# Computing the adaLN modulation of a two-layer hybrid backbone with the weight blocks stationary

## The reference, cut to what matters

```python
mod = jax.nn.silu(cond) @ ada_w + ada_b          # ada_w: (1024, 3072) per layer, float32
shift, scale, gate = jnp.split(mod, 3, axis=-1)
h = rms_norm(x, norm_g) * (1.0 + scale[:, None, :]) + shift[:, None, :]
# ... h @ w_in feeds a gated recurrence, a differential attention and a Fourier mixer ...
x_new = x + gate[:, None, :] * (merged @ w_out)
```

## Time and profile before

| what | value |
|---|---|
| median of 3 runs | 3388.12 us (3386.97 to 3388.16) |
| the profiled execution's own time | 3383.91 us |
| its span, first to last instruction | 3381.9 us |
| mean granted clock of TensorE | 0.979 |
| PE busy | 3139.2 us, 93% |
| PEld busy | 2976.2 us, 88% |
| DVE, ACT, POOL busy | 1296.2, 1073.8, 690.0 us |

### The profile page before, as it was taken

One profiled execution on the slowest core, in us unless ns is written; L12 is line 12 of the kernel. 1 busy time (PEld: TensorE's weight loads), 2 busy tenths in 40 slices (PEclk: granted clock), 3 DMA queues, 4 the chain that ended last, 5 costly groups with the idle time before them and its releaser, 6 DMA issues.

```text
span 3381.9 us, 43875 instructions
## 1 busy us (share of the span) xinstructions
PE 3139.2 (93%) x18496; PEld 2976.2 (88%) x18496; DVE 1296.2 (38%) x1769; ACT 1073.8 (32%) x2022; POOL 690.0 (20%) x404
## 2 busy tenths in 40 slices
PE   5798889899999999999988988989999999999999
PEld 1388888898898999999988888979889899999999
DVE  1253455356564211121335445435656431022121
ACT  1332333356654311010123333345656432011010
POOL 0021112111111123333331111111111112233332
PEclk9899999999999999999999999999999999999999
DMA  8301000100101111211330100110000020121131
GB/s 321 126 26 42 30 30 27 50 21 28 36 22 48 55 32 47 66 46 40 131 122 27 36 30 27 34 50 21 29 30 22 26 76 29 47 67 46 41 110 68
DMA packets 52115, 182.58 MB, mean 54 GB/s; under 512 B 5584, under 2 KB 12752, under 8 KB 49232
## 3 DMA queue, kind: packets, MB, share of 16 engines
q1 hardware_dynamic: 28800, 92.29, 8.9%
q10 hardware_dynamic: 23120, 87.49, 6.8%
HBM read 149.35 MB, written 30.41 MB: 53 GB/s over the span
## 4 chain that ended last, share of the span: by engine, by line
PE 80%; DVE 9%; ACT 5%; DVEq 3%; issue 2%; ACTq 1%; DMA 1%
PE ps L319 59%; PE ps L530 3%; PE ps L373 3%; PE ps L504 2%; PE ps L505 2%; PE ps L517 2%; DVE a_at L1291 1%; PE ps L421 1%; DVE stat L1407 1%; DVEq L1283 1%; PE ps L586 1%; PE ps L468 1%; DVE a_q L1280 1%; ACT a_at L808 1%; DVE b_qs L1387 1%
## 5 line engine op out<-in xcount | busy, mean ns | idle before, releaser
L319 PE MATMUL ps<-h_hi,w_hi 128*128 128x384 f32 x3648 | 1240.2, 340 | 50.3 <-DVE h_lo L1237 25.7
L319 PE MATMUL ps<-h_hi,w_lo 128*128 128x384 f32 x3648 | 1225.6, 336 | 0.0
L319 PE MATMUL ps<-h_lo,w_hi 128*128 128x384 f32 x3648 | 1225.2, 336 | 0.0
L319 PEld LDWEIGHTS ps<-h_hi,w_hi 128*128 128x128 f32 x3648 | 690.0, 189 | 59.6 <-issue 58.0
L679 POOL CAST w_hi<-w_raw 128x1024 fp32r<-128x1024 f32 x200 | 197.2, 986 | 2650.4 <-PE ps L319 2645.4
L319 PEld LDWEIGHTS ps<-h_hi,w_lo 128*128 128x128 f32 x3648 | 690.0, 189 | 2.0 <-issue 1.0
L319 PEld LDWEIGHTS ps<-h_lo,w_hi 128*128 128x128 f32 x3648 | 689.7, 189 | 0.0
L681 POOL TENSOR_TENSOR w_lo<-w_raw,w_hi 128x1024 fp32r<-128x1024 f32 x200 | 492.6, 2463 | 16.0
L1074 ACT ACTIVATE m_g<-ps 128x384 f32<-128x384 f32 x144 | 70.7, 492 | 763.7 <-PE ps L319 753.7
L1407 DVE TENSOR_REDUCE stat<-ps 128x1 f32<-128x1152 f32 (+1 forms) x144 | 177.8, 1235 | 227.9 <-PE ps L505 227.9
L1489 DVE TENSOR_TENSOR m_p<-ps,m_g 128x384 f32<-128x384 f32 x96 | 53.5, 558 | 476.3 <-PE ps L319 476.3
(11 more groups left out here) (218 smaller groups left out, 3567.5 us busy)
## 6 DMA issues: line engine op xcount, KB each, us to landing
w_raw<-in_w_full SPq DMA_DIRECT2D x152, 512.0 KB, 3.5
ada_slabs<-in_ada_w ACTq DMA_DIRECT2D x16, 1536.0 KB, 8.8
w_raw<-in_w_half SPq DMA_DIRECT2D x48, 256.0 KB, 2.6
x_res<-x_keep ACTq DMA_DIRECT2D x16, 576.0 KB, 8.1
out_x_new<-X ACTq DMA_DIRECT2D x16, 576.0 KB, 2.8
X<-in_x_t ACTq DMA_DIRECT2D x1, 4608.0 KB, 18.0
x_keep<-X ACTq DMA_DIRECT2D x1, 4608.0 KB, 13.3
y_keep<-X ACTq DMA_DIRECT2D x8, 576.0 KB, 3.0
```

The costliest lines, as they stand in the source:

```text
L319: mm = pe.matmul(ps[:, bank, 0:TILE], w[:, slot, k, :], r[:, k, cols_of(t)], start=(k == 0 and i == 0), stop=(k == kt - 1 and i == 2))
```

## The change

The operands of the modulation's matmuls are exchanged. A 128x128 block of the slab is stationary, and the two columns of `cond` move. Output block j of layer l lands at once with its channels on the partitions, in columns 2j and 2j + 1 of bank 6 + l, where the 24 blocks of the layer accumulate over its eight slabs. For each slab there are 24 matmuls in place of six. The copies to `mod_row`, the transposes, the buffer, and the semaphores `ada_row`, `ada_t` and `setup_done` go, and with them PE's wait between the layers. DVE waits for `ada_mm` at 8 and 16.

```diff
-    mod_row = at("mod_row", [2, 3 * D_MODEL], F32, off_s + 1024)
...
             for l in range(DEPTH):
-                if l:
-                    pe.wait_ge(ada_row, l)
                 for k in range(KD):
                     s = l * KD + k
                     pe.wait_ge(slab_in[s % 6], 16 * (s // 6 + 1))
-                    for n in range(6):
-                        mm = pe.matmul(ps[0:2, n, :], cond[:, k, :], slabs[:, s % 6, n * 512:(n + 1) * 512],
-                                       start=(k == 0), stop=(k == KD - 1))
+                    for j in range(3 * KD):
+                        mm = pe.matmul(ps[:, 6 + l, 2 * j:2 * j + 2], slabs[:, s % 6, j * P:(j + 1) * P],
+                                       cond[:, k, :], start=(k == 0 and j == 0), stop=(k == KD - 1 and j == 3 * KD - 1))
                     mm.then_inc(ada_mm, 1)
-                pe.wait_ge(ada_row, l + 1)
-                if l:
-                    pe.wait_ge(setup_done, l)
-                for j in range(3 * KD):
-                    mm = pe.transpose(ps[:, 6, 2 * j:2 * j + 2], mod_row[0:2, j * P:(j + 1) * P],
-                                      sq_c[0:2, IDENT, 0:2])
-                mm.then_inc(ada_t, 1)
...
                 if s >= 6:
                     act.wait_ge(ada_mm, s - 5)
-                if s == KD + 5:
-
-                    act.activation(mod_row[:, :].rearrange("p (a b) -> p a b", a=6), ps[0:2, 0:6, :],
-                                   ACT.Copy).then_inc(ada_row, 1)
                 act.dma_start(slabs[:, s % 6, :], ada_w[s // KD, (s % KD) * P:(s % KD + 1) * P, :]).then_inc(slab_in[s % 6], 16)
-            act.wait_ge(ada_mm, DEPTH * KD)
-            act.wait_ge(ada_t, 1)
-            act.activation(mod_row[:, :].rearrange("p (a b) -> p a b", a=6), ps[0:2, 0:6, :],
-                           ACT.Copy).then_inc(ada_row, 1)
             act.wait_ge(lb_sub, 1)
...
-                dve.wait_ge(ada_t, l + 1)
+                dve.wait_ge(ada_mm, KD * (l + 1))
                 ab = par[:, PC_AB + l * 24:PC_AB + (l + 1) * 24].unsqueeze(2).broadcast_to((P, 24, 2))
-                dve.tensor_tensor(mod[:, l, :, :], ps[:, 6, 0:48].rearrange("p (j c) -> p j c", c=2), ab,
-                                  ALU.add).then_inc(setup_done, 1)
+                dve.tensor_tensor(mod[:, l, :, :], ps[:, 6 + l, 0:48].rearrange("p (j c) -> p j c", c=2), ab,
+                                  ALU.add)
```

More of the change, by code:

```diff
@@ L229, in mixer_kernel @@
         tile_free = [sem(f"tile_free{t}") for t in range(NT)]
-        cond_ready, ada_mm, ada_row, ada_t, setup_done, eps_set = (
-            sem(n) for n in ("cond_ready", "ada_mm", "ada_row", "ada_t", "setup_done", "eps_set"))
+        cond_ready, ada_mm, eps_set = (sem(n) for n in ("cond_ready", "ada_mm", "eps_set"))
         lam_dot, lam_exp, lb_sub, lb_exp = (sem(n) for n in ("lam_dot", "lam_exp", "lb_sub", "lb_exp"))
```

## The result

The changed kernel took 3448.33 us (median of 4 runs, 3448.22 to 3448.86) against 3387.57 us before (4 runs, 3386.97 to 3388.16). The ratio is 1.0182, with a 95% interval of 1.0170 to 1.0194: 60.8 us slower, where 64.0 us were forecast.

What follows compares the result with a forecast made beforehand. PE, busy 93% of the span, was taken as the bound. At half clock 163.8 + 0.3 + 0.8 = 164.9 us replace 100.9 us, +64.0 us: 3388.1 us becomes 3452.1 us, range 3438 to 3470 us.

Steps and rivals of the forecast that it cites:

- The price of a pair: Modulation stream on PE: each of 768 load-and-matmul pairs takes 0.2133 us at half clock, 163.8 us in all.
- The nearest rows: Trace streams of ordinary 128x128 blocks, 128 columns moving, taken as pace: 0.1115 us at full, 0.213 us at half clock.
- The reading of the loads' durations: PE loads: above a fixed part, an ordinary float32 block takes 106 ns, a transposing one 53 ns.
- The 337 ns of the upper bound: Modulation stream: if no load hid behind a matmul, each pair takes the load's 337 ns at half clock, 259 us.
- the rival built on it: Modulation stream: float32 loads cost no more than transposing ones; skill's 107 ns gives 82 us; 13.0 us less, chance 0.04.
- The clock: PE's granted clock: begins the modulation stream at 0.50 and stays there until the first projection.
- the likeness to the two-column transposes: Modulation stream looks like the transposes, at 0.50 throughout 142 to 144 us, so its clock would not rise.
- What was removed: Between layers and in the tail: copies, transposes, exponentials leave the path, up to 14.0 us; 0.8 us stay.
- their cover at about 5 us: Tail: lbt to lam_n and layer 0's mod hide under the last slabs' matmuls; uncovered they would cost 5 us.
- What moved: DMA: x_keep, 13.3 us, is issued earlier beside the last slabs; costed at nothing, with 32 us of cover.
- the carry-over to the median: Whole kernel: the profiled execution's 4.2 us under the median is carried over, so 3388.1 + 64.0 = 3452.1 us.
- the uncertainty that the prediction named: Later in the kernel: stretches at 0.50 may fall elsewhere against the work, some us either way.

Runs made afterwards that it cites:

- half_load: The changed kernel loading only 64 columns of each 128x128 block, the other 64 channels' modulation left at the bias; 3370.57 us, ratio 0.9948 to the kernel before.
- wide64: The changed kernel with 64 columns moving in each modulation matmul, 62 of them zeros; 3453.34 us, ratio 1.0191 to the kernel before.
- old_exp_early: The kernel before with ACT's two exponentials moved ahead of its wait for the last slab; 3381.52 us, ratio 0.9983 to the kernel before.
- warm_start: The changed kernel with eight unread float32 matmuls of 384 columns on PE ahead of the stream; 3444.14 us.
- exp_late: The changed kernel with ACT's exponentials put back behind the last slab; 3450.78 us in one execution.
- wide64_warm: wide64_filled with eight matmuls of 384 columns put ahead of the stream; 3371.20 us in one execution.
- wide128: The changed kernel with 128 filled columns moving, six banks a layer, layer 1 waiting for DVE's read, exponentials earlier; 3373.93 us, ratio 0.9959 to the kernel before.
- wide16: The changed kernel with 16 columns moving in each modulation matmul; 3452.15 us in one execution.
- packed: Against the changed kernel: condition stationary again, each slab's six matmuls spread over three column groups, one copy and eight transposes a layer, exponentials early; 3339.02 us.
- packed_early: packed with three slabs' modulation ahead of the norm's sums, SiLU ahead of the squares, slabs 6 to 8 issued earlier; 3331.76 us, ratio 0.9834 to the kernel before.
- wide64_filled: wide64 with the two condition columns repeated 32 times in place of zeros; 3452.34 us in one execution.

## Why the prediction was right, point by point

*The price of a pair* was the whole question, and it was 0.2135 us for 0.2133 forecast; the stream 163.98 us for 163.8. The nearest rows, streams of ordinary blocks with 128 columns moving at half clock, were the right ones. `half_load` and `wide64` show why they carry over: the load's columns set the pace, and 2 or 64 columns moving behind it do not. The arithmetic was looser than it reads, though. The two starts in the earlier trace rows give (262.91 - 262.48) / 2 = 0.215 us and not 0.213; the 0.2133 that was multiplied is 256 cycles at 1.2 GHz and stands in no row. With 0.215 the stream would have been forecast at 165.1 us, 1.1 us too long.

*The reading of the loads' durations* held for the float32 blocks: 64 columns at 0.50 are 0.107 us, which is 128 cycles at 1.2 GHz, two for each column. That a transposing block takes half of that was read from its rows alone; no run tested it. The 337 ns of the upper bound was taken for a load at half clock, which the earlier trace rows do not say; the changed kernel's loads last 333 ns at 0.50. The Trainium skill's figure (TensorE: Matmul & The Clock Gate, section "LDWEIGHTS (loading the stationary operand)") gives, as an estimate, 53 ns for these 64 columns and 107 ns for 128; for float32 blocks the trace shows twice that at 0.50 and about that at 1.00, so the rival built on it fell.

*The clock* stayed at 0.50 from the start of the stream to the projection, as forecast. That it began there was read from the kernel before, with the same idle time ahead. That it would not rise was argued from the likeness to the two-column transposes, and the row that this rested on does not carry it: by the window of 142 to 144 us the clock had long fallen, while PE sat idle, and in `old_exp_early` the same 24 transposes ran at 1.00. The fall at 91 us, with idle time and transposes ahead of it, left both causes open. The first two lines are of the kernel before, the last two of `old_exp_early`:

```profile
139.00:140.00 1.00, 0.00 (x0) 0.00 (x0) 0.70 (x7) 0.00 (x0) 0.00 (x0) 0.71 1.03 419
140.00:141.00 1.00, 0.00 (x0) 0.00 (x0) 0.81 (x7) 0.00 (x0) 0.00 (x0) 0.50 0.99 401
...
136.00:137.00 1.00, 0.66 (x11) 0.67 (x11) 0.00 (x0) 0.28 (x1) 0.00 (x0) 1.00 1.01 401
137.00:138.00 1.00, 0.97 (x16) 0.89 (x15) 0.00 (x0) 0.00 (x0) 0.00 (x0) 1.00 1.03 419
```

So here the forecast was right with some luck. What it claimed was shown only afterwards, by `warm_start`: with two columns moving the level falls without any idle time. The advice of the same page of the Trainium skill (section "Why this matters for your kernels") that continuous work gives TensorE its full clock is not borne out by this stream, which ran at 0.50 for 164 us without a gap.

*What was removed* came out as forecast: 0.82 us between the last matmul and `n_t` for 0.8. That `lbt` to `lam_n` and the `mod` of layer 0 hide is in the trace (they end by 151 us). I priced their cover at about 5 us, which was too much: `exp_late` gives 3.0 us in this kernel, and `old_exp_early` 4.0 us in the kernel before, without the transposes' clock.

*What moved* cost nothing that the trace shows; `x_keep` took 18.1 us to land in place of 13.3, with nobody waiting.

*The term that was off most* is the carry-over to the median. The profiled execution before lay 4.2 us under its median, and I added that to the forecast; that of the changed kernel, 3448.22 us, lies with the rest of its runs. Against the trace the forecast was 3447.9 us for 3448.2, against the median 3452.1 for 3448.33. The +64.3 us between the profiled executions is +60.8 us between the medians, and the 64.0 us lie so near to the first of them because the two profiled executions have nearly the same part behind `n_t` (3237.3 and 3238.0 us).

Where such differences come from can be read in part. Behind `n_t` the clock stood at 0.50 for 123 to 126 us of the traces of the kernel before, `old_exp_early`, `wide64_warm` and `wide128`, whose rest lasts 3236.8 to 3238.7 us, and for 143 to 148 us of `wide64`, `wide16`, `packed` and `packed_early`, whose rest lasts 3241.0 to 3243.9 us. Likewise the executions of the kernel before that took under 3386 us have a mean clock of 0.979 or 0.980, and those above 3389 us one of 0.975 to 0.977. That is the uncertainty that the prediction named (stretches at 0.50 that fall elsewhere). What decides it is not shown.

What stays open is why the streams differ. Of those that started at 0.50, the ones with 2, 16 and 64 columns moving stayed there and the one with 128 rose, as did the stream of the kernel before with 512 (0.69 in its window of 46 to 48 us); of those that started at 1.00, the one with 2 fell and the one with 64 stayed. `warm_start` and `wide64_warm` are one execution each. No rule follows from them.

## What to carry to other kernels

An exchange of operands that takes columns off the moving side puts them on the loads; the number of weight columns that pass through the array, 3072 for each slab in two records each either way, did not change here. So at the full clock there was nothing to win in the stream: 85.96 us (`wide64_warm`) against 192 x 0.429 = 82.4 us for the old records. Ask of any stream with much loading and little moving what the granted clock does in the nearest like stretch: here that factor of two was 78 us, and the removal of every copy, transpose and wait around it about 14. The thin operand can also stay stationary and its matmuls be spread over column groups of the array; here the transfer of the weights was then the bound.

## What the hardware showed that I had not expected

- The same instructions ran for 164 us at 0.50 (`wide64_filled`) or for 86 us at 1.00 (`wide64_warm`), by what eight matmuls, 5 us of work, had done before. This stream kept the level that it found; the one with two columns moving did not (`warm_start`).
- Matmuls on three column groups overlapped almost fully, in float32 too: 1.92 us for what takes 5.1 us one after another, where a third of that would be 1.7 us.
- DMA held 418 to 433 GB/s from 50 to 82 us beside them, without a visible cost to PE: the twelve records of a slab took 1.92 us beside it, and 1.92 us for the last slab (87.58 us), when DMA moved 12 GB/s.
- In `packed` the clock also went to 0.50 for some us (0.64 in the window of 62 to 66 us, 0.50 in that of 66 to 70 us), at a time when PE waited for slabs. It cost little, since the transfer was the bound.
- At the very start the profile's clock is not borne out by the pace. In the kernel before, the norm's matmuls of 384 columns start 0.64 us apart where the clock reads 1.00, and their loads last 0.34 us, as those of the changed kernel do at 0.50. In `warm_start` 16 records of the same shape take 5.16 us, 0.32 us each, at 1.00. The levels that the argument above rests on agree with the pace of their pairs (0.2135 us at 0.50, 0.112 us at 1.00).

```profile
33.88 0.34 PEld L354 LDWEIGHTS ps<-n_acc,sq_c 128*128 128x128 f32 x1 [0.30 <-issue]
34.52 0.34 PEld L354 LDWEIGHTS ps<-n_acc,sq_c 128*128 128x128 f32 x1 [0.30 <-issue]
...
34.00:36.00 2.00, 2.00 (x5) 1.09 (x4) 0.27 (x1) 0.00 (x0) 0.00 (x0) 1.00 0.98 412
```
